# Seven products for half of the FFN's up rows, none for its down tiles, in a two-part transformer block in fp32

## The reference, cut to what matters

```python
D_FF = 2816
def rmsnorm(x, g):
    y = xf * lax.rsqrt(jnp.mean(xf * xf, axis=-1, keepdims=True) + EPS)
    return y * g
def conv_ffn(x, w_up, w_conv, b_conv, w_down):
    h = causal_dwconv(x @ w_up, w_conv, b_conv)     # 1024 -> 5632, three taps along the tokens
    gate, val = jnp.split(h, 2, axis=-1)
    return (jax.nn.silu(gate) * val) @ w_down       # 2816 -> 1024
for layer in range(2):
    ...
    h = h + conv_ffn(rmsnorm(h, ffn_norm_g[layer]), ffn_w_up[layer], ffn_conv_w[layer], ffn_conv_b[layer], ffn_w_down[layer])
```

## Time and profile before

| | |
|---|---|
| median of 3 runs | 1978.5 us (1978.48 to 1978.77) |
| the profiled execution, and its span from first to last instruction | 1975.7 us, 1973.9 us |
| mean granted clock of TensorE | 0.986 |
| TensorE matmul / weight load busy | 96% / 80% |
| VectorE / ScalarE / GpSimd busy | 61% / 48% / 42% |
| FFN of layer 0, of layer 1 | from 1057 us, from 1600 us |
| chain that ended last | TensorE 77%, VectorE 16%, ScalarE 3% |

### The profile page before, as it was taken

How to read it: one execution, slowest core, us unless ns; L and a number is a source line. 1 busy time by engine, 2 the same in 40 slices (tenths; PEclk the granted TensorE clock), 3 DMA queues, 4 the chain that set the end, 5 groups by cost and what they waited for, 6 DMA issues and landing times.

```text
span 1973.9 us, 31122 instructions
## 1 busy us (share of the span) xinstructions
PE 1886.8 (96%) x12229; PEld 1581.5 (80%) x12229; DVE 1211.3 (61%) x1721; ACT 945.3 (48%) x1307; POOL 835.4 (42%) x597
## 2 busy tenths in 40 slices
PE   5999999998999999979899999999999999999997
PEld 4888888886878888758648888887888888888876
DVE  6123777775267656878996656456834456664568
ACT  4344777776256555452435453344433344533543
POOL 1323222234221112143524557656744545675565
PEclk8999999999999999989999999999999999999999
DMA  8111112114111111222112323222322322223222
GB/s 314 68 64 43 63 55 108 55 55 161 54 65 41 55 55 54 69 91 72 59 50 79 106 86 107 98 95 86 114 90 96 107 81 101 93 100 107 86 92 69
DMA packets 49121, 169.87 MB, mean 86 GB/s; under 512 B 5584, under 2 KB 7888, under 8 KB 48976
## 3 DMA queue, kind: packets, MB, share of 16 engines
q1 hardware_dynamic: 46672, 163.07, 23.5%
q10 hardware_dynamic: 2304, 4.81, 0.7%
HBM read 165.77 MB, written 2.10 MB: 85 GB/s over the span
## 4 chain that ended last, share of the span: by engine, by line
PE 77%; DVE 16%; ACT 3%; issue 2%; DMA 1%; POOL 0%; ACTq 0%; SPq 0%; DVEq 0%
PE ps L686 23%; PE ps L687 22%; PE ps L688 22%; PE ps L824 3%; PE ps L843 2%; ACT sq L1298 2%; DVE wS L1858 2%; DVE cv L1858 2%; DVE X L1858 1%; DVE wS L2387 1%; DMA raw<-in_units 1%; PE ps L727 1%; DVE tmp L1858 1%; DVE hf L1858 1%; DVE X L1864 1%
## 5 line engine op out<-in xcount | busy, mean ns | idle before, releaser
L1841 POOL TENSOR_TENSOR wlo<-raw,whi 128x512 fp32r<-128x512 f32 x486 | 658.8, 1383 | 843.3 <-ACT whi L1259 806.0
L686 PE MATMUL ps<-Bhi,whi 128*128 128x512 f32 (+1 forms) x948 | 360.5, 380 | 1.6 <-POOL wlo L1841 1.6
L687 PE MATMUL ps<-Blo,whi 128*128 128x512 f32 (+1 forms) x948 | 361.0, 381 | 0.0
L688 PE MATMUL ps<-Bhi,wlo 128*128 128x512 f32 (+1 forms) x948 | 357.7, 377 | 0.0
L1259 ACT ACTIVATE whi<-raw 128x1024 fp32r<-128x1024 f32 x208 | 214.4, 1057 | 273.8 <-PE ps L688 261.4
L686 PEld LDWEIGHTS ps<-Bhi,whi 128*128 128x128 f32 x948 | 177.9, 188 | 39.0 <-issue 2.7
L688 PEld LDWEIGHTS ps<-Bhi,wlo 128*128 128x128 f32 x948 | 178.0, 188 | 34.7
L687 PEld LDWEIGHTS ps<-Blo,whi 128*128 128x128 f32 x948 | 178.2, 188 | 33.3 <-issue 0.7
L1864 DVE SCALAR_TENSOR_TENSOR cv<-ps,vec,cv 128x511 f32<-128x511 f32 (+1 forms) x176 | 131.9, 749 | 70.8 <-ACT cv L1298 66.2
L1858 DVE TENSOR_TENSOR ps<-ps,rstd 128x1024 f32<-128x1024 f32 (+1 forms) x60 | 69.7, 1162 | 167.8 <-PE ps L688 135.1
L686 PE MATMUL ps<-Fhi,whi 128*128 128x512 f32 (+1 forms) x393 | 135.5, 345 | 3.4 <-POOL wlo L1841 3.0
(11 more groups left out here) (319 smaller groups left out, 4385.2 us busy)
## 6 DMA issues: line engine op xcount, KB each, us to landing
raw<-in_units SPq DMA_DIRECT2D x301, 512.0 KB, 3.3
X<-in_xT SPq DMA_DIRECT2D x4, 512.0 KB, 8.5
X<-in_xT ACTq DMA_DIRECT2D x4, 512.0 KB, 5.7
out_xT<-X SPq DMA_DIRECT2D x8, 256.0 KB, 2.2
CX<-in_ctxT SPq DMA_DIRECT2D x4, 256.0 KB, 8.7
acc<-in_rope ACTq DMA_DIRECT2D x1, 384.0 KB, 2.9
gmw<-in_gmw ACTq DMA_DIRECT2D x1, 384.0 KB, 3.2
bs<-in_bs ACTq DMA_DIRECT2D x1, 384.0 KB, 3.7
```

Of the source, the lines that this page charges most:

```text
L686: nc.tensor.matmul(out, sh, mh, start=first, stop=False, skip_group_check=beside)
L687: nc.tensor.matmul(out, sh, ml, start=False, stop=False, skip_group_check=beside)
L688: return nc.tensor.matmul(out, sl, mh, start=False, stop=last, skip_group_check=beside)
L1841: lo = nc.gpsimd.tensor_tensor(wlo[:, s % CONV, cols], raw[:, plan.unit_at[("split", s)] % RAW, cols], whi[:, s % CONV, cols].bitcast(fp32 ...
```

## The change

- The down tiles are all plain again. `summed` of down weights, the sums of rows and their splits go; the parts are two of 11 rows. Down units are freed when their last tile is done and no longer inside a tile.
- Of each layer's 22 up rows nine are done by seven products: rows 4, 6, 8, 10 of part 0, and 1, 3, 5, 7, 9 of part 1. The 2 x 2 block is now (first or second half of the 1024 input channels) x (gate or value), against (half of the channels) x (half of the tokens). Such a row uses two units of weights, A and B, and two sums: C (1024 columns, `sum_13`) and E (512 columns, `sum_2`); `sum_4` is added in place in B. VectorE makes these in the rows before (`summed` for row 4 behind row 2, for row 1 of part 1 ahead of row 0, for the others inside the seven-product row before), and three steps on results follow during and after the products (`first_sum`, `middle_sums`, `last_sum`).
- The input of these rows must be divided by the root mean square beforehand: VectorE builds it (`forms`: X times gain times `rstd`, and sums of halves) and ScalarE splits it to `Zhi`, while GpSimd and VectorE (`forms_low`) make `Zlo`. This is done for one of four pairs of channel blocks k at a time, ahead of and in rows 0, 1 and 2 of part 0. Rows 0 to 3 stay as they were (with `scaled`); the plain rows after them read the new input and need no scaling.
- The norm's ones-matmul stands after the gate half of the first tile of each FFN and of the mixer between them, not behind the whole tile.

```diff
+PLAIN = 4
+SEVENS = [(l, f, j) for l in range(2) for f in range(2) for j in range(FH) if j % 2 == f and (f or j >= PLAIN)]
 # TensorE
+            def seven(u):
+                l, f, j = SEVENS[u]
+                y, x = opened(("ub", u), True), opened(("ua", u), True)
+                r6, r3, r7 = (y[:, i * HT:(i + 1) * HT] for i in range(3))
+                r1, r4, r5 = (x[:, i * HT:(i + 1) * HT] for i in (0, 2, 3))
...
+                multiply("A", 0, X11, r1).then_inc(sem("f1"), 1)
+                multiply("A", 1, T4, r4).then_inc(sem("fa"), 1)
+                multiply("E", 0, T2, r6).then_inc(sem("fv"), 1)
+                multiply("C", 0, T3, r7)
+                multiply("C", 1, T1, r5).then_inc(sem("fq"), 1)
+                pe.wait_ge(sem("fV"), u + 1)
+                done(multiply("B", 0, X22, r3), ("ub", u))
+                pe.wait_ge(sem("c1"), u + 1)
+                done(multiply("B", 1, X21, r1, True), ("ua", u))
 # ScalarE
+            def forms_high(l, k):
+                y, z = ty[:, k % 2, :, :], HK * l + k
+                ac.wait_ge(sem("zy"), 2 * z + 2)
+                act(Zhi[:, X11:X12 + 1:X12 - X11, k, :], y[:, 0, :].rearrange("p (i t) -> p i t", i=2), ACT.Copy, sem_name="zh")
+                act(Zhi[:, X21:X22 + 1, k, :], y[:, 1, :].rearrange("p (i t) -> p i t", i=2), ACT.Copy, sem_name="zh")
+                ac.wait_ge(sem("zt"), 3 * z + 3)
+                act(Zhi[:, T1:T4 + 1, k, :], Tf[k % 2], ACT.Copy, sem_name="zth")
+            def classic_row(l, f, r, u):
...
+                if u is not None:
+                    convert_to(plan.pair_of["B", u])
...
+                row_part(l, f, r, gate, 0)
+                row_part(l, f, r, val, 1)
+                if f == 0 and r + 1 < PLAIN:
+                    forms_high(l, r + 1)
+                if u is not None:
+                    first_part(u)
+                    convert_to(plan.pair_of["B", u] + 1)
+                silu(l, f, r, gate, 2)
+                high(Fhi[:, r, :], val)
             def ffn(l):
                 for f in range(2):
+                    for r in range(FH):
                         if f == r == 0:
+                            convert_to(val_unit(l, 1))
                             root(f"ffn{l}")
+                            forms_high(l, 0)
+                        if (l, f, r) in SEVENS:
+                            seven_row(SEVENS.index((l, f, r)))
+                        else:
+                            classic_row(l, f, r, SEVENS.index((l, f, r + 1)) if (l, f, r + 1) in SEVENS else None)
+                        if f == 0 and r + 2 < PLAIN:
+                            convert_to(val_unit(l, r + 2))
+                        if (l, f, r + 2) in SEVENS:
+                            convert_to(plan.pair_of["C", SEVENS.index((l, f, r + 2))])
 # VectorE
+            def forms(l, k):
+                y, t, z = ty[:, k % 2, :, :], Tf[k % 2], HK * l + k
...
+                made = [mark(STTi(y[:, i, :], X[:, k + HK * i, :], v_(f"ffn_g{l}", k + HK * i), rstd[:, 0:T], MUL, MUL), "zy")
+                        for i in range(2)]
+                need(*made)
...
+                need(mark(TTi(t[:, 0:2, :], x12, x11_22, SUB), "zt"))
+                need(mark(TTi(t[:, 2, :], y[:, 1, HT:T], t[:, 0, :], SUB), "zt"))
+                need(mark(TTi(t[:, 3, :], y[:, 1, 0:HT], t[:, 2, :], SUB), "zt"))
+            def classic_row(l, f, r, u):
+                plain = f == 0 and r < PLAIN
+                if f == r == 0:
...
+                    forms(l, 0)
+                    forms_low(l, 0)
+                ps = psum(("up", l, f, r))
...
+                if plain:
+                    scaled(ps, "scaled")
+                    if r + 1 < PLAIN:
+                        forms(l, r + 1)
...
+                if plain and r + 1 < PLAIN:
+                    forms_low(l, r + 1)
+                if u is not None:
+                    first_sum(u)
+                gated(l, f, r, gate, val)
+                if u is not None:
+                    middle_sums(u)
+                flush()
+                if u is not None:
+                    last_sum(u)
...
+            def seven_row(u):
...
+                taps(u)
+                if after:
+                    sum_13(after)
+                gated(l, f, r, x[:, 0:T], y[:, T:2 * T])
+                if after:
+                    sum_2(after)
+                flush()
+                if after:
+                    sum_4(after)
```

More of the change, by code:

```diff
@@ L379, in ffn @@
+            for i, part in enumerate(("A", "E", "C", "B")):
+                self.part[len(self.split) // UT + i] = (part, u)
+                self.pair_of[part, u] = len(self.split) // UT + i
+            weights = block(0, gate) + block(1, val) + ["summed"] * (2 * UT) + block(0, val) + block(1, gate)
+            row = (2 * l + f) * FH + j
+            tile(("ub", u), [("c12", u + 1), low_of(row)])
+            tile(("ua", u), [("c12", u + 1), ("c2", u + 1), ("hf", hf_of(row))], weights)
         def ffn(l):
@@ L1166, in ffn @@
             def ffn(l):
                 for f in range(2):
-                    for j in range(FR[f]):
-                        tile(("up", l, f, j))
-                        for part in range(2):
-                            last = linear(("up", l, f, j), Bhi, Blo, 0, SAT[f"ffn{l}"] + 1, XO, offset=KD * part,
-                                          ks=list(range(KD)), col0=T * part, halved=None if part else 1)
-                        done(last)
-                        if f == j == 0:
-                            norm(f"ffn{l}")
@@ L1176, in ffn @@
-                    end = FR[f] - 1
+                    for j in range(FH):
+                        if (l, f, j) in SEVENS:
+                            seven(SEVENS.index((l, f, j)))
+                            continue
+                        first = f == j == 0
+                        ps = opened(("up", l, f, j), True) if first else tile(("up", l, f, j))
+                        for part in range(2):
+                            if f == 0 and j < PLAIN:
+                                last = linear(("up", l, f, j), Bhi, Blo, 0, SAT[f"ffn{l}"] + 1, XO, offset=KD * part,
+                                              ks=list(range(KD)), col0=T * part, halved=None if part else 1)
+                            else:
+                                last = from_forms(ps[:, part * T:(part + 1) * T], ("up", l, f, j), KD * part)
+                            if part == 0:
+                                last.then_inc(sem("gate"), 1)
+                                if first:
+                                    norm(f"ffn{l}")
+                        done(last, ("up", l, f, j) if first else None)
@@ L1185, in ffn @@
                         done(last)
-                    units = list(plan.groups[l, f])
-                    for p in range(1, 4):
-                        if p in SEVENS[l, f]:
-                            while not ended:
-                                seven(l, f, units.pop(0))
-                            assert ended.pop() == p
-                            continue
-                        for m in range(2 * p, min(2 * p + 2, 8 - l * f)):
-                            tile(("dn", l, f, m))
-                            done(linear(("dn", l, f, m), Fhi, Flo, 0, SAT[f"act{l}{f}"] + 1, XO, halved=m % 2 or None))
+                    for m in range(2, 8 - l * f):
+                        tile(("dn", l, f, m))
+                        done(linear(("dn", l, f, m), Fhi, Flo, 0, SAT[f"act{l}{f}"] + 1, XO, halved=m % 2 or None))
@@ L1246, in convert @@
                     s = converted[0]
-                    if s in plan.part or s >= CONV and plan.last[("split", s - CONV)] > n:
+                    was = plan.freed_by[s]
+                    if s in plan.part or (was is not None and plan.last[("split", was)] > n):
                         break
@@ L1260, in convert, with freed @@
                     converted[0] += 1
                     split_at.append(n)
+            def freed(s):
+                was = plan.freed_by[s]
+                part, u = plan.part.get(was, (None, None))
+                if was in plan.used:
+                    ac.wait_ge(sem("used"), plan.used[was])
+                    return
+                if was in plan.gate_unit:
+                    ac.wait_ge(sem("gate"), plan.gate_unit[was])
+                    return
+                if part in ("A", "E", "C"):
+                    ac.wait_ge(sem({"A": "fa", "E": "fv", "C": "fq"}[part]), u + 1)
+                elif was is not None:
+                    ac.wait_ge(sem("psum"), plan.last[("split", was)] + 1)
```

586 lines of the change are left out of this document (291 added, 295 removed).

## The result

The changed kernel takes 1989.95 us (median of 4 runs, 1987.91 to 1992.85) against 1978.49 us in the same session (1977.36 to 1978.77): ratio 1.0063, 95% interval 1.005 to 1.0076. By the medians that is +11.5 us. The profiled execution is 1990.5 us, its span 1988.7 us, 14.7 us above the 1973.9 us of before (by the unrounded times): the profiled execution of before lies 2.8 us under its median, that of the changed kernel 0.6 us above its own. The prediction had +22.0 and 2000.5 us. Two of the six runs of hollow_forms (2639 and 3850 us) and one of the kernel before beside it (2012.5 us) fell in a slow state and are in no number here; all other runs were fast.

A forecast was written before the change was run, and what follows sets the result against it. TensorE bounds the kernel, a matmul in flight for 96% of 1973.9 us. -20.0 + 11.8 - 8.0 + 1.0 + 0.8 + 32.4 + 4.0 = +22.0 us gives median 2000.5; own range 1990 to 2010, widened toward the rivals to 1986 to 2012.

The forecast's parts named there:

- Sign and mechanism: Rows 0 to 4 of part 0: slower, as VectorE's forms delay ScalarE's splits and TensorE waits three times; slower 85%, forecast 72%.
- Waits: TensorE in rows 2 to 4 of each layer waits 4.1, 3.9 and 8.2 us: 16.2 a layer, +32.4 us.
- half clock: TensorE's clock drops behind the 8.2 us wait: 2 us a layer, +4.0 us, bounds 0 and +8.
- Seven-product rows: 18 up rows of 84 matmuls of 256 columns, 9.91 us against 11.01 plain: -20.0 us.
- the rival of starving rows: Hand-overs eat the 1.2 us of cover; TensorE waits 1 us in each of 18 seven-product rows: 2018 us, 12%.
- Down tiles: Old seven-product saving given back +11.8 us, waits for weights gone -8.0, down units just in time +1.0.
- the 1.0: Down units, freed only at a tile's end, arrive just in time without cover: +1.0 us over four parts, bounds 0 and +4.
- The norm: Ones-matmul after the first tile's gate half: no wait for ffn0 or ffn1, sum 0.8 us late for mix1, +0.8 us.
- The plain rows keep up: Rival: VectorE's forms fit between the rows and units come when wanted; -14.4 us, 1964 us, 8%.
- The limit: Waits of a layer, clock included, below which the rival of plain rows keeping up decides: 7.2 us.
- The forms miss POOL: Rival: SBUF-only operations run at least times, 6.4 us of waits a layer, hardly a clock drop; about 1978 us, no change, 7%.
- a weight load shows between halves: Rival: weight loads add 84 x 0.19 us to a seven-product row, over +250 us for 18 rows; 1%.

The follow-up runs named there:

- hollow_forms: Changed kernel with VectorE's `forms` mostly left out for two of the four k (64 of 512 columns, 32 of 256): 1984.7 us, ratio 1.0039 to the kernel before.
- small_lows: Changed kernel with POOL making only 128 of 1024 columns of the low parts of six units a layer: 1973.6 us, ratio 0.9982 to the kernel before.
- splits_ahead: Changed kernel with ScalarE's splits of the next value units and unit A ahead of Silu in rows 0 to 2: 1983.5 us, ratio 1.0042 to the kernel before.
- first_six: Changed kernel with row 6, not 4, first by seven products and `summed` behind row 4: 1977.6 us, ratio 1.0004 to the kernel before.
- best: Changed kernel with row 6 first by seven products, earlier splits, `summed` behind row 3, row 4's ready k pairs first: 1971.3 us, ratio 0.9971 to the kernel before.
- a_before: Changed kernel with value splits ahead of Silu and A's split ahead of the rounding of the last forms: 1985.3 us, ratio 1.0044 to the kernel before.
- hollow_before: Changed kernel with both the shortened forms of hollow_forms and the earlier splits of a_before: 1979.1 us, ratio 1.0016 to the kernel before.

## Why the prediction was right, point by point

*Sign and mechanism.* Right. VectorE's forms lengthen rows 0 to 2, ScalarE's splits stand behind each row's copy, and TensorE waits three times. The order worked out met the trace closely. Counted from the start of the FFN (1057.48 us in the prediction, 1058.55 in the profile), row 1's and row 2's copies on ScalarE were to end after 43.0 and 56.0 us and ended after 42.4 and 55.1; row 4 was to start after 61.1 us and started after 60.2. small_lows (collisions and shorter pieces of POOL), splits_ahead (place) and first_six (a later first seven-product row) each took away their share of the waits.

*Size, term by term.*
- Waits: 16.2 us a layer predicted, 4.1 + 3.9 + 8.2; measured 3.7 + 2.0 + 8.0 with 1.65 us of half clock behind the first. A drop there was to be swallowed by the next wait, and it was: 2.0 + 1.65 is 3.7 against 3.9. The eight-microsecond waits cost 2.6 and 1.7 us of clock, against 4.0 for both. Together 34.9 against 36.4.
- Seven-product rows: -20.0 predicted (18 x 1.10 is 19.8), -24.0 measured. The step of 0.118 us was read in one stretch. Matmuls of 256 columns step by 0.113 in some stretches and by 0.118 in others, in both kernels and whatever they read; most of the new ones met the shorter step. Two such rows, start and the start of the next row (timeline of PE after), and old products in layer 1 (timeline of PE before, 10 steps):

```profile
1142.09 0.28 PE L644 MATMUL ps<-Zhi,whi 128*128 128x256 f32 x1
1142.20 0.28 PE L645 MATMUL ps<-Zlo,whi 128*128 128x256 f32 x1
...
1151.69 0.39 PE L644 MATMUL ps<-Zhi,whi 128*128 128x512 f32 x1
...
1264.40 0.28 PE L644 MATMUL ps<-Zhi,whi 128*128 128x256 f32 x1
...
1274.32 0.39 PE L644 MATMUL ps<-Zhi,whi 128*128 128x512 f32 x1
```
```profile
1748.56 0.28 PE L686 MATMUL ps<-T,whi 128*128 128x256 f32 x1
...
1749.70 0.28 PE L687 MATMUL ps<-T,whi 128*128 128x256 f32 x1
```

  9.60 us for 84 in the one and 9.92 in the other, where 9.91 was predicted. No idle inside: the rival of starving rows did not come. The plain rows on two-block forms cost nothing more, 48 matmuls in 10.99 us.
- Down tiles: +4.8 predicted (11.8 - 8.0 + 1.0), +1.2 measured. Units freed at a tile's end arrived in time (60.55 us a part, 88 x 0.688, no wait), so the 1.0 did not come. The products themselves gave up about 13 us, more than the 11.8, since a part of the old ones had the step of 0.113. But two losses went with the old tiles that the sum had put at nothing. The old tiles stalled for 0.1 to 0.3 us at a time, mostly where they go from `T` to `Fhi`, too short for the view of waits; about 2.6 us in all. One of these in the trace before:

```profile
1391.35 0.28 PE L688 MATMUL ps<-T,wlo 128*128 128x256 f32 x1
1391.76 0.38 PE L686 MATMUL ps<-Fhi,whi 128*128 128x256 f32 x1
1391.98 0.28 PE L687 MATMUL ps<-Flo,whi 128*128 128x256 f32 x1
```

  And of the 3.3 us at the very end one wait went: TensorE was idle for 1.15 us ahead of the ones-matmul at 1960.30 before, and not at all ahead of the same one at 1974.43 after, which is 1.4 us from start to start.
- The norm: 0.8 us predicted for mix1, 0.85 measured at 1434.67. The mixer grew by 1.2 us; its 256-column matmuls step by 0.118 in this trace and partly by 0.113 in the one before.

So the terms that were off most are the saving of the seven-product rows and the price of the down tiles; both erred toward slower. Against the spans the sum was 7.3 us too high: 4.0 of the seven-product rows, 3.6 of the down tiles and 1.5 of waits and clock, less 1.8 that it did not have (1.1 ahead of the FFN, 0.4 in the mixer, 0.3 behind the last matmul). Against the medians it was 10.5 us too high, +22.0 for +11.5. The measured 1989.95 us lies just outside the forecast's own 1990 to 2010; the wider 1986 holds it because it reached toward the rivals. The mechanism and the waits were right on their own account; that the number fell in the range owes something to that room.

*The rivals.* "The plain rows keep up" would need waits, clock included, below 7.2 us a layer. The changed kernel has 18.0 and 17.0 us, best 6.6 and 5.6, and best is faster than before. The limit itself was too low, since rows and tiles gave 7 us more than predicted: with the measured terms it is 10.8 us for nine seven-product rows a layer and 9.5 for eight. first_six has about 10.4 and 10.3 us and comes out level. "The forms miss POOL" is nearly what small_lows builds (its units are also ready sooner): 7.3 us a layer are left, near the rival's 6.4, with 1.5 and 1.9 us of clock behind them. It is 3.5 us faster than before by its ratio of 0.9982, where the rival had no change, again because of the limit. That a weight load shows between halves was refuted again (a plain row has 51 loads by the prediction's own count, not the 48 of its estimate): the Trainium skill's page TensorE: Matmul & The Clock Gate, Part 3 (What overlaps and what doesn't), has loads overlap only across row groups, and by that rule a step of 0.114 us with a load of 0.19 us for each matmul could not be. The same Part 3 of the Trainium skill's page, in The mechanism, also lets a load into a background weight buffer be pulled ahead; with that the step is no contradiction, but no trace here shows where a load goes.

*What the experiments corrected.* I took the 8.0 us before row 4 for one delay, A's split behind the copy. It is three ends of the one VectorE chain in series: the forms' low parts, A's low part on a POOL that also serves the forms, and E's sum. Removing one uncovers the next (splits_ahead, hollow_forms, a_before, hollow_before). The forms alone are the smallest of them: their last low part ended at 1112.23 in the changed kernel, 1.5 us after PE stood ready for row 4, and first_six, which reads them in row 4 all the same, waits 1.4 us there. The rest is what only a seven-product row asks for, A behind the copy and the sums of weights behind the gating; it went when that row stood two rows later.

## What to carry to other kernels

A prologue that must be finished before a cheaper form can run is to be costed against the PE work that lies ahead of the first instruction that needs each part of it. Here VectorE's chain ran from 1068 to 1114 us where four rows of TensorE would have ended at 1103, and cost 17 us a layer with its clock. Two plain rows put between the end of the forms and the first seven-product row covered most of it, for one saved row of 1.3 to 1.4 us: the plain rows need the new input alone, the seven-product row also its sums of weights. Moving a split past a Silu, or one operand ahead of another, gains only until the next end of the same chain; find the last of them before pricing the first. Where VectorE reads two SBUF operands, moving POOL's work earlier may only change what it collides with.

## What the runs showed of the hardware

- VectorE's operations on two SBUF operands beside POOL's low parts: a 256-column add 1.38 us and not 0.42, a 512-column one 1.59 and not 0.69, and at their least again once POOL's pieces are 0.32 us (small_lows). That agrees with the Trainium skill, SBUF — State Buffer, Who interferes with whom, which has a `tensor_tensor` with both inputs in SBUF contend with GpSimd's reads.
- Matmuls of 256 columns, each with its own load of 0.19 us, step by 0.113 us or by 0.118, for whole stretches at a time and whatever they read: products from `T` by 0.118 at 1207 us and 0.113 at 1748 before, products from `Zhi` by 0.113 at 1142 us and 0.118 at 1264 after. The products of E step by 0.120 (12 in 1.44 us). What sets the difference stays open; it costs 0.3 us in a row of 84, and a step read in one stretch does not price another.
- In the changed kernel the granted clock was 0.50 for 3.4 us after idle of 3.6 to 3.7 us, and around an idle of 8.0 us for 10.2 us in layer 0 and 6.8 in layer 1, of which 5.7 and 3.6 lay on work. The same wait cost 2.6 us in one layer and 1.7 in the other. Shorter idle was followed by it too, but not each time: in best an idle of 2.0 us that ended at 1122.74 and one of 2.6 that ended at 1641.59 by 3.4 us at 0.50, another of 2.6 us that ended at 1104.01 by none.
